# A two-block transformer kernel: pre-norm weights as columns, a reordered head loop, and diagonal convolution taps issued ten at a time

## The reference, cut to what matters

```python
for i in range(DEPTH):
    h = rms_norm(x, pre_norm_g[i])
    ...                                   # i == 0: retention, h @ w_in first
ya = a_val * jax.nn.sigmoid(a_gate)       # 512 channels
ya = causal_dwconv(ya, w_dw_a[l], b_dw_a[l])   # 31 taps for each channel
ya = jax.nn.silu(layer_norm(ya, ln_a_g[l], ln_a_b[l]))
```

## Time and profile before

| | |
|---|---|
| median of three runs | 875.16 us |
| time of the profiled execution | 875.0 us |
| its span | 873.2 us |
| TensorE matmul busy | 858.1 us, 98% |
| VectorE busy | 662.8 us, 76% |
| ScalarE busy | 492.7 us, 56% |
| GpSimd busy | 50.3 us, 6% |
| granted TensorE clock, mean | 0.996 |

### The profile page before, as it was taken

One profiled execution on the slowest core, in us unless ns is written; L12 is line 12 of the kernel. 1 busy time (PEld: TensorE's weight loads), 2 busy tenths in 40 slices (PEclk: granted clock), 3 DMA queues, 4 the chain that ended last, 5 costly groups with the idle time before them and its releaser, 6 DMA issues.

```text
span 873.2 us, 15801 instructions
## 1 busy us (share of the span) xinstructions
PE 858.1 (98%) x5676; PEld 781.1 (89%) x5676; DVE 662.8 (76%) x928; ACT 492.7 (56%) x732; POOL 50.3 (6%) x61
## 2 busy tenths in 40 slices
PE   9999999999999999999999999999999999999995
PEld 7898999988868999999988889999998999999884
DVE  6869777686865786877866876899898788888566
ACT  5454545544646656656565446455753698888440
POOL 0018000000012000000000000070000000000000
PEclk9999999999999999999999999999999999999998
DMA  7857575669554656473738662634444465556541
GB/s 245 307 190 236 191 247 176 232 234 340 177 178 156 227 168 233 132 254 112 259 121 319 230 220 85 208 120 146 145 157 181 134 228 176 184 184 228 193 166 48
DMA packets 48433, 169.60 MB, mean 194 GB/s; under 512 B 5507, under 2 KB 6147, under 8 KB 48390
## 3 DMA queue, kind: packets, MB, share of 16 engines
q1 hardware_dynamic: 40612, 142.70, 48.2%
q10 hardware_dynamic: 7778, 26.32, 8.4%
HBM read 167.95 MB, written 1.05 MB: 194 GB/s over the span
## 4 chain that ended last, share of the span: by engine, by line
PE 87%; DVE 8%; ACT 2%; issue 2%; ACTq 0%; POOL 0%; DVEq 0%; POOLq 0%
PE bank L445 14%; PE bank L446 14%; PE bank L447 14%; PE bank L491 8%; PE bank L493 8%; PE bank L492 8%; PE bank L458 3%; PE bank L534 2%; PE bank L858 2%; DVE wlo L1441 1%; PE bank L766 1%; PE bank L654 1%; PE bank L655 1%; PE bank L656 1%; PE bank L769 1%
## 5 line engine op out<-in xcount | busy, mean ns | idle before, releaser
L934 ACT ACTIVATE whi<-raw 128x1024 fp32r<-128x1024 f32 (+1 forms) x251 | 259.6, 1040 | 223.7 <-PE bank L447 106.7
L1441 DVE TENSOR_TENSOR wlo<-raw,whi 128x1024 fp32r<-128x1024 f32 (+1 forms) x251 | 301.8, 1212 | 91.8 <-ACT whi L934 89.4
L445 PE MATMUL bank<-H,whi 128*128 128x256 f32 x904 | 261.6, 289 | 0.0
L447 PE MATMUL bank<-H,wlo 128*128 128x256 f32 x904 | 255.7, 283 | 0.0
L446 PE MATMUL bank<-H,whi 128*128 128x256 f32 x904 | 255.6, 283 | 0.0
L445 PEld LDWEIGHTS bank<-H,whi 128*128 128x128 f32 x904 | 173.2, 192 | 1.0 <-issue 0.4
L446 PEld LDWEIGHTS bank<-H,whi 128*128 128x128 f32 x904 | 173.3, 192 | 0.5
L447 PEld LDWEIGHTS bank<-H,wlo 128*128 128x128 f32 x904 | 173.1, 192 | 0.0
L491 PE MATMUL bank<-whi,Y 128*128 128x512 f32 x216 | 84.2, 390 | 0.0
L493 PE MATMUL bank<-whi,Y 128*128 128x512 f32 x216 | 84.1, 389 | 0.0
L492 PE MATMUL bank<-wlo,Y 128*128 128x512 f32 x216 | 84.1, 389 | 0.0
(11 more groups left out here) (259 smaller groups left out, 1310.6 us busy)
## 6 DMA issues: line engine op xcount, KB each, us to landing
ada_raw<-ada_in ACTq DMA_DIRECT2D x48, 512.0 KB, 5.2
raw<-w_head SPq DMA_DIRECT2D x47, 512.0 KB, 4.5
raw<-w_up SPq DMA_DIRECT2D x42, 512.0 KB, 3.4
raw<-w_down SPq DMA_DIRECT2D x22, 512.0 KB, 4.2
raw<-w_uq SPq DMA_DIRECT2D x24, 384.0 KB, 3.1
raw<-w_ret_out SPq DMA_DIRECT2D x16, 512.0 KB, 4.9
raw<-w_ple_gate SPq DMA_DIRECT2D x16, 512.0 KB, 4.6
raw<-w_mla_gate SPq DMA_DIRECT2D x16, 512.0 KB, 4.9
```

The costliest lines, as they stand in the source:

```text
L445: mm(o, whi[:, s, c], a[:, 0, :], start=start, stop=False)
L447: last = mm(o, wlo[:, s, c], a[:, 0, :], start=False, stop=stop)
L934: activation(whi[:, s, 0:n], block_in(b, n), ACT.Copy).then_inc(hi_done, 1)
L1441: tt(wlo[:, s, 0:n], block_in(b, n), f32(whi[:, s, 0:n]), ALU.subtract).then_inc(lo_done, 1)
```

## The change

Beginning. The norm weights of the first layer arrive as a 128x8 tile of columns, `pre`, behind the identity matrix on ScalarE's queue. The row and its spreading are gone, and with them VectorE's wait. VectorE multiplies X by the reciprocal alone. The weights go in while the turned chunks are copied: four operations of 128 columns with a scale on each of ScalarE and VectorE for each tile, each with its own semaphore step. TensorE runs 20 holds in one go. `split(B_HEAD + 2)` comes ahead of the sine on both engines.

Head loop. The splits of a pass are j = 3 to 14. The first rotary step stands at the head of a pass, the `ada` steps stand behind the splits j = 4, 6, 8 and 9, and the mask stands ahead of `split(B_HEAD + 8)`. Modulation weights are loaded one at a time.

Convolution. Eight taps of tile 2 (k = 3, 5, and 7, 11 + 8i for i = 0, 1, 2) go from VectorE to the diagonals. They are summed in the second half of bank M3 and added by VectorE at the end. 39 diagonal taps are issued as 6 behind four strips of pool_in, 10 behind each four strips of gates, and 3 at the end. `DG` has 16 places in the two buffers `ada_raw`.

```diff
+DIAG_FIRST = [(0, 3), (1, 3), (2, 3), (3, 3), (4, 3), (3, 2)]
+DIAG_PASS = [(5 + k, 3) for k in range(8)] + [(7, 2), (11, 2)]
+DIAG_LAST = [(5, 2), (29, 3), (30, 3)]
+N_TAPS = 3 * CONV_K - 8
...
-        DG = WK[:, 13:15, :].rearrange("p a t -> p (a t)").rearrange("p (r m) -> p r m", r=4)
+        DG = ada_raw[:].rearrange("p a n -> p (a n)").rearrange("p (r m) -> p r m", r=16)
...
             pe.wait_ge(const_ready, 1)
-            hold(PB[1], 4)
-            pe.wait_ge(row_a, 16)
-            for h in range(2):
-                last = mm(PB[0][:, 512 * h:512 * h + 512], ones[0:1, :], ROW_A[0:1, 512 * h:512 * h + 512], start=True,
-                          stop=True)
-            last.then_inc(row_spread, 1)
-            hold(PB[1], 3)
+            hold(PB[1], 20)
...
-            plain_strip(B_HEAD, first[0], 0, [(plain_a, 1)] + [None] * 3 + [(plain_d, 1)])
+            plain_strip(B_HEAD, first[0], 0, [(plain_a, k + 1) for k in range(4)] + [(plain_d, k + 1) for k in range(4)])
...
+            def diagonals(taps, n0, i=0):
+                for n, (k, c) in enumerate(taps):
+                    pe.wait_ge(tap_ready, n0 + n + 1 + 10 * i)
+                    first, last = (k, c) in (DIAG_FIRST[0], DIAG_FIRST[5]), (k, c) in (DIAG_LAST[0], DIAG_LAST[2])
+                    x = CI[:, c, bass.ds(k + 8 * i, T)]
+                    mm(M1[:, 0:T] if c == 3 else M3[:, T:2 * T], DG[:, (n + (4 if n0 == 0 else 0)), :], x, start=first,
+                       stop=last).then_inc(conv_sum, 1)
             for j in range(4):
                 if j % 2 == 0:
                     b = free_a(A_WP + j // 2)
                 strip(B_WP + j, halves(b)[j % 2], H)
-                for k in ((), (0, 1), (2, 3), (4,))[j]:
-                    tap(k)
+            pe.wait_ge(dve_free, V_WA + 4 + 2)
+            diagonals(DIAG_FIRST, 0)
             with pe.Fori(0, 3) as i:
                 for j in range(4):
                     if j % 2 == 0:
                         b = free_a(A_WG + j // 2, 2, i)
                     strip(B_WG + j, halves(b)[j % 2], H, 4, i)
-                    for k in (5 + 2 * j, 6 + 2 * j):
-                        tap(k, i, 8)
-            tap(29)
-            tap(30)
+                diagonals(DIAG_PASS, 6, i)
+            diagonals(DIAG_LAST, 36)
...
-            act.dma_start(ROW_A[0:1, :], rows_in[R_PRE0].unsqueeze(0)).then_inc(row_a, 16)
             act.dma_start(ident[:], ident_in).then_inc(in_ident, 16)
+            act.dma_start(pre[:], pre_in).then_inc(in_pre, 16)
...
-                activation(WT[:, t, 0:512], b[:, 0:512], ACT.Copy).then_inc(plain_a, 1)
+                for k in range(4):
+                    activation(WT[:, t, P * k:P * k + P], b[:, P * k:P * k + P], ACT.Copy, scale=pre[:, k:k + 1])\
+                        .then_inc(plain_a, 1)
...
             split(B_HEAD + 1)
+            split(B_HEAD + 2)
             act.wait_ge(trig_arg, 1)
...
-            dve.wait_ge(row_spread, 1)
             for t in range(2):
                 inverse_of(t + 1, t)
-                pre_rows(t, PB[0][:])
+                ts(WT[:, t, :], X[:, t, :], rs[:, t, 0:1], None, ALU.mult).then_inc(wt_ready, 1)
+            dve.wait_ge(in_pre, 16)
             for t in range(2):
                 dve.wait_ge(turned_psum, 2 * t + 2)
-                nc.vector.tensor_copy(WT[:, t, 512:1024], PB[2 + t][:, 512:1024]).then_inc(plain_d, 1)
+                for k in range(4, 8):
+                    ts(WT[:, t, P * k:P * k + P], PB[2 + t][:, P * k:P * k + P], pre[:, k:k + 1], None, ALU.mult)\
+                        .then_inc(plain_d, 1)
...
             ts(rt, rt, PI_IN, -PI_IN, ALU.min, ALU.max).then_inc(trig_arg, 1)
+            split(B_HEAD + 2)
             dve.wait_ge(trig_ready, 1)
...
-                for j in range(2, 12):
-                    split(B_HEAD + j, 1024, 12, i)
-                    if j == 2:
-                        used(B_HEAD + 1, 12, i)
-                        rope(GD[0], TA, TB, 0, Q, 1, dve_free, V_HEAD + 3, rope_ready, 2, (2, 2, 4), i)
...
+                used(B_HEAD + 1, 12, i)
+                rope(GD[0], TA, TB, 0, Q, 1, dve_free, V_HEAD + 3, rope_ready, 2, (2, 2, 4), i)
+                for j in range(3, 12):
                     if j == 8:
                         dve.wait_ge(at_ready, i + 1)
                         m = maskd[:, bass.ds(i, 1), :].rearrange("p a t -> p (a t)")
                         tt(AT[:, 0:T], M2[:, 0:T], m, ALU.mult).then_inc(atm_ready, 1)
                         tt(AT[:, T:T + P], M2[:, T:T + P], m[:, 0:P], ALU.mult).then_inc(atm_ready, 1)
+                    split(B_HEAD + j, 1024, 12, i)
...
-                split(B_HEAD + 12, 1024, 12, i)
-                split(B_HEAD + 13, 1024, 12, i)
+                for j in range(12, 15):
+                    split(B_HEAD + j, 1024, 12, i)
...
                 for c in range(3):
+                    if (k, c) in ON_PE:
+                        continue
...
-            dve.wait_ge(conv_step, 3 * CONV_K)
+            dve.wait_ge(conv_step, N_TAPS)
+            dve.wait_ge(conv_sum, N_DIAG + 4)
+            tt(CO[:, 2, :], CO[:, 2, :], M3[:, T:2 * T], ALU.add).then_inc(conv_step, 1)
```

More of the change, by code:

```diff
@@ L55 @@
 NCOLS = _n
[L59 removed]
+R_POST0, R_PRE1, R_QKV, R_POST1, R_LN1G, R_LN1B, R_LN2G, R_LN2B = range(8)
 B_HEAD = 0
@@ L626, in _ @@
             first = halves(free_d(V_HEAD))
-            plain_strip(B_HEAD, first[0], 0, [(plain_a, 1)] + [None] * 3 + [(plain_d, 1)])
+            plain_strip(B_HEAD, first[0], 0, [(plain_a, k + 1) for k in range(4)] + [(plain_d, k + 1) for k in range(4)])
             plain_strip(B_HEAD + 1, first[1], 0)
-            plain_strip(B_HEAD, first[0], 1, [(plain_a, 2)] + [None] * 3 + [(plain_d, 2)])
+            plain_strip(B_HEAD, first[0], 1, [(plain_a, k + 5) for k in range(4)] + [(plain_d, k + 5) for k in range(4)])
             plain_strip(B_HEAD + 1, first[1], 1)
@@ L940, in load_ada @@
             def load_ada(x, per, i):
[L942 to L945, removed]
+                n = x % 2
+                act.wait_ge(ada_used, x + 1 + per * i)
+                act.dma_start(ada_raw[:, n, :], ada_in[bass.ds(per * i + x, 1)].rearrange("b p n -> p (b n)"))\
+                   .then_inc(ada_loaded[n], 16)
             tables = [0]
@@ L1297, in _, with diagonal @@
             act.wait_ge(in_ident, 16)
[L1299 to L1304, removed]
+            def diagonal(taps, n0, n, i=0):
+                slot = n + (4 if n0 == 0 else 0)
+                if n0 > 6 or n0 == 6 and n > 3:
+                    act.wait_ge(conv_sum, n0 + n - 10 + 1 + 4 + 10 * i)
+                elif n0 == 6:
+                    act.wait_ge(conv_sum, n + 1 + 10 * i)
+                k, c = taps[n]
+                activation(DG[:, slot, :], ident[:], ACT.Copy, scale=dcol("dwa", CONV_K * c + k + 8 * i)).then_inc(tap_ready, 1)
+            act.wait_ge(lo_done, RING + B_WA + 6)
             for j in range(4):
                 split(B_WP + j)
-                for k in ((0, 1), (2, 3), (4, 5), (6,))[j]:
-                    tap(k)
+                for n in ((0, 1), (2, 3), (4, 5), ())[j]:
+                    diagonal(DIAG_FIRST, 0, n)
                 if j == 2:
@@ L1315, in _ @@
                     split(B_WG + j, 1024, 4, i)
-                    for k in (7 + 2 * j, 8 + 2 * j):
-                        tap(k, i, 8)
+                    for n in ((0, 1, 2), (3, 4, 5), (6, 7), (8, 9))[j]:
+                        diagonal(DIAG_PASS, 6, n, i)
                     if j == 2:
@@ L1320, in _ @@
                 evac(B_WG + 3, 1, dyn(G, 4 * i + 2, 2), ACT.Sigmoid, 4, i)
-            act.wait_ge(conv_sum, CONV_K)
+            for n in range(3):
+                diagonal(DIAG_LAST, 36, n)
+            act.wait_ge(conv_sum, N_DIAG + 4)
             activation(CO[:, 3, :], M1[:, 0:T], ACT.Identity, bias=col("bdwa", 3)).then_inc(conv_last, 1)
@@ L1702, in _ @@
                         tt(AT[:, T:T + P], M2[:, T:T + P], m[:, 0:P], ALU.mult).then_inc(atm_ready, 1)
+                    split(B_HEAD + j, 1024, 12, i)
+                    if j == 4:
+                        used(B_HEAD + 3, 12, i)
+                        rope(GD[1], TA, TB, 0, K, 2, dve_free, V_HEAD + 4, rope_ready, 4, (2, 2, 4), i)
+                    if j == 4:
+                        ada(0, 0, 0, 4, i)
+                    if j == 6:
+                        ada(1, 1, 0, 4, i)
+                    if j == 8:
                         ada(2, 0, 1, 4, i)
@@ L1721, in _ @@
                 tt(dyn(Yl, 4 * i, 4), YF, f32(dyn(Yh, 4 * i, 4)), ALU.subtract).then_inc(y_ready, 1)
-                split(B_HEAD + 12, 1024, 12, i)
-                split(B_HEAD + 13, 1024, 12, i)
+                for j in range(12, 15):
+                    split(B_HEAD + j, 1024, 12, i)
             mod_read(0, 0, 2, GD[1])
             p_lo(0)
-            out_rows(B_RO, 16, 3, ROW_A, 32)
+            out_rows(B_RO, 16, 3, ROW_A, 16)
             gate_start(B_PJ0, B_PG0, U_PLE0, X_PLE0, False)
```

65 lines of the change are left out of this document (31 added, 34 removed).

## The result

| | before | after |
|---|---|---|
| median of 9 runs each | 875.53 us | 879.61 us |
| lowest to highest | 874.96 to 876.49 | 877.69 to 881.86 |
| profiled execution, span | 875.0, 873.2 | 879.79, 878.0 |

The ratio is 1.0047, 95% interval 1.0038 to 1.0057: the change costs 4.1 us, 3.3 to 5.0. The forecast was 874.7 us in a range that ended at 877.0. One of the 11 runs of e9 took 1206.43 us at a granted clock of 0.657 and is left out of its ratio.

The account below looks back on a forecast made before the run. TensorE was taken as the limit outside the beginning, which VectorE partly sets up to 31.58 us. The terms -2.9 - 0.7 + 3.5 - 0.3 = -0.4 us on 875.0, plus 0.16 to the median, gave 874.7 us, range 873.6 to 877.0.

Parts of the forecast that it names:

- Part 1: Beginning: first split strip 2.6 us earlier, block 6 near 28.7 instead of 31.58 us, 2.9 us gained in all.
- the middle between two bounds: Beginning: holds end at 5.9 us at the upper clock level, 9.9 at the lower; 7.9 taken.
- The new load: Beginning: load of the norm weight columns, there between 4.3 and 6.7 us, needed at 9; costs nothing, up to some tenths.
- Part 2: Head loop: 0.7 us gained by the earlier mask; the other moves taken as 0, with 0.5 us lost as bound.
- 0.7 for the mask: Second head: mask ahead of the second split ends TensorE's wait, 0.7 us gained, bounds 0 and 0.7.
- Part 3: Convolution: eight more taps at 0.432 us lose 3.5 us, the wait at the mean gives 0.3 back; grouping gains nothing.
- 0.3 us at the mean: Convolution: TensorE's wait for the last VectorE tap at the mean goes, 0.3 us gained.
- Rival 1: Beginning: clock stays low through the holds, which loses 0.2 us instead of gaining 2.9; 877.8 us, chance 0.12.
- Rival 2: Convolution: each change between split strips and taps costs 0.18 us, 11 fewer groups save 2.0; 872.7 us, chance 0.06.
- rival 3: Convolution: weights arrive late in strips without taps, 2 to 4 us a pass with GpSimd; about 878 us, chance 0.03.
- 0.5 us for the moved loads: Head loop: modulation loads behind the third split, needed a block or more later; taken as 0, bound 0.5 us lost.

Follow-up runs that it names:

- e9: Kernel before with the new head loop, its modulation loads issued ahead of the third split; beginning and convolution of before: 874.14 us, ratio 0.9985.
- e7: e5 with 7 holds instead of 20 at the start: 873.32 us, ratio 0.9972.
- e2: Kernel before with the new beginning alone (columns, 20 holds, chunked copies): 874.78 us, ratio 0.9986.
- e8: Kernel after, late loads kept, with VectorE's modulation steps 16 and 17 behind splits j = 3 and 4 in ret_out: 878.69 us, ratio 1.0036.
- e3: Kernel before with the new convolution alone: 879.35 us, ratio 1.0045.
- e5: e4 with the convolution of before: 871.46 us, ratio 0.9962.
- e4: Kernel after with the modulation loads issued ahead of the third split again: 874.89 us, ratio 0.9990.
- e6: Kernel before with its own 31 diagonal taps issued in groups of 5, 8 and 2, none moved from VectorE: 876.10 us, ratio 1.0003.
- e1: Kernel before with the new head loop alone, old beginning and old convolution: 878.61 us, ratio 1.0028.

## Why the prediction was wrong, point by point

**Part 1, right in size.** Expected at the first split strip were 2.6 us and at block 6 2.9; measured are 2.58 and 3.06. e7 shows that the holds carry it. The holds end at 8.5 us, where I had taken 7.9 as the middle between two bounds; that the clock rose within them was a guess that came true. (TensorE is at the lower level only to near 13 us before, by the distances of the earlier trace rows, not up to 31.58 us as the prediction's first paragraph has it.) The new load cost nothing. The Trainium skill, "DMA: Bandwidth & Descriptors", section Specifications, had spoken against it with its 512 bytes: the columns, 32 bytes a partition, took 5.6 us from an issue at 1.17 us. They were there at 6.8 and wanted at 9.05, by ScalarE's first copy; the identity with its 64 KB took 4.8 us in the same run, so no row shows a penalty that mattered. What I missed is that this gain stands only on the new order of the splits (e2): I had booked all of it to the beginning.

**Part 2, its gain about right, its cost wrong. This is the step that failed.** From block 6 to the first modulation matmul after gains 1.1 us, where I had 0.7 for the mask. The traces show 0.94 of it between the norms of the first and the second head (49.70 to 90.20 us before, 46.50 to 86.06 after), where the mask stood: the wait of 0.71 us and a slower first matmul behind it. The other 0.14 lies in the first head. The failed words are: "the ScalarE list now holds the sine and the next modulation loads behind the third split of the next stage, which waits for one more block of TensorE. They are needed a block or more later. I take 0, with 0.5 us lost as the other bound." The change was seen, and so was what the split waits for, but neither number had a row under it. In after VectorE is free for the first load 2.8 us after its issue (182.05 - 179.26). That is indeed about a block of TensorE, which takes 2.7 us here, but no slack: the load needed 3.1 us even alone, before, and 7.0 here. I had priced a late load as its own lateness. It costs 5.4 us, by three things that the timelines, e8 and the queues' rows show: it falls behind the weight loads, VectorE and ScalarE both hold splits behind it, and the splits that stand still delay the weight loads after it. How the 5.4 us divide between the three no run shows. The trace of before had rows to bound it by. The load used at 184.12 had landed only 0.3 us earlier, and VectorE already idled for a later one:

```profile
206.75 1.29 DVE L1457 SCALAR_TENSOR_TENSOR ada_acc<-ada_raw,siluc,ada_acc 128x1024 f32<-128x1024 f32 x1 [1.84 <-DMA ada_raw<-ada_in]
```

**Part 3, right.** Predicted +3.2 us, measured +3.4 in after, e3 and e5 against e4. The loop of gates takes 15.83 us a pass (predicted 15.8), and no weight block was late. Ten taps take 4.3 us: from 581.25 to the second strip matmul at 585.69, less 0.12. Taps moved to TensorE are a plain loss here: TensorE waits for nothing in this stretch but 0.3 us at the mean.

**The rivals.** Rival 1, the low clock, didn't come in the five executions with 20 holds: their first split strips start between 17.01 and 17.33 us. No run shows its price as it was meant. The nearest is e7: with fewer holds the transposes stay at 0.21 us apart, and the first split strip comes 2.5 us later, where the rival had 3.2. Rival 2 is refuted by e6, rival 3 by the absence of such waits in after and e3. The cause that came was in none of them.

**The range.** Its upper end, 877.0, rested in part on 0.5 us for the moved loads. A term with no row, on a queue whose next user stands at the head of another engine's list, should have had a bound of several us: the length of the stall it can cause on that engine, not the time by which it moves.

## What to carry to other kernels

When a block of an in-order list is moved past others, look up for each DMA issue behind it when it goes out, what it goes out next to on the other queue, and which engine has its landing at the head of its list. Where loads of two queues serve the same engine, the urgent one belongs ahead of the other's burst. An early start is worth only what the next engine's order lets through, so two changes that each look small can be worth more together: 0.7 and 1.7 us alone at the first modulation matmul, 4.3 together. And in a stretch bound by TensorE, work given to TensorE is paid in full; here grouping it changed nothing.

## What the runs showed of the hardware

The same two 512 KB loads landed 3.1 and 4.0 us after their issues when they went out 1.7 us ahead of the weight loads, and 7.0 and 10.5 us after them when the weight loads began to go out 1.0 us ahead.

The moment at which the clock rises isn't the same in each run of the same code. With the beginning of before, the 16 transposes took 3.65 us in the kernel before, and 2.97 us in e3:

```profile
8.87 2.97 PE L542 MATMUL bank<-ident,Z 128*128 128x128 f32 x16
```

In e3 and e9 the first split strip came at 18.75 and 18.86 us, in before, e1 and e6 at 19.6 to 19.8, with the same code of TensorE up to there. One profiled execution can be up to 1 us off for this reason alone.

The clock also fell behind short waits, but not in each execution. In e8, TensorE's matmuls of 512 columns lie 0.43 us apart for 3.7 us behind the wait of 2.37 us, where they lie 0.23 us apart at 2.4 GHz; about 1.7 us go there besides the wait. The granted clock of these 3.5 us is 0.51, which is the level of 1.2 GHz (the row of TensorE: stretch, length, busy, granted clock, DMA share, GB/s):

```profile
203.20:206.70 3.50, 3.50 (x9) 0.51 0.82 290
```

In after the wait of 2.7 us had no such stretch behind it. Why the one and not the other I can't say.

The same thing explains most of what e2 and e4 lose from 250 us to the holds near 665 us against before and after in turn (0.96 and 0.79 us), where no edit lies. In the norm near 250 us TensorE waits 0.57 us ahead of eight transposes and 1.07 us behind them, in e2 and e4 as in before and after. In e2 and e4 the matmuls of 512 columns then lie 0.43 us apart for 3.4 us, and the next transposes come 0.9 us later than in the other two. The same row of e2:

```profile
252.20:256.20 4.00, 3.97 (x11) 0.57 0.39 131
```

Why these two executions and not the others stays open.
